# Router of a mixture-of-experts layer: rows scaled and turned by transposes, matmuls of 256 and 320 columns, ranks inside the shared block, gather behind the selectors

## The reference, cut to what matters

```
h = rms_norm_2(x, g_ffn_norm) * (1.0 + scale_f) + shift_f
def moe_ffn(h, w_router, b_router, w_exp_gate, w_exp_up, w_exp_down, w_sh_gate, w_sh_up, w_sh_down):
    scores = jax.nn.sigmoid(xf @ w_router)                 # 256 tokens x 64 experts
    choice = scores + b_router
    group_score = top_k(choice by 8 groups of 8, 2).sum     # keep the 4 best groups
    expert_idx = top_k(choice inside the kept groups, 6)
    gate = scores[expert_idx] / their sum * 2.5
    ...
    # every expert block (64 experts, each 1024 -> 256 -> 1024)
    hb = silu(xb @ w_exp_gate[e]) * (xb @ w_exp_up[e]);  y = (hb @ w_exp_down[e]) * g
    shared = (silu(xf @ w_sh_gate) * (xf @ w_sh_up)) @ w_sh_down
    return shared + routed
```

## Time and profile before

| | us |
|---|---|
| median of 3 runs | 1116.52 |
| lowest and highest | 1115.83 and 1118.21 |
| the profiled execution | 1116.18 |
| its span, first to last instruction | 1114.5 |
| TensorE busy | 1060.0 (95%) |
| VectorE busy | 560.6 (50%) |
| ScalarE busy | 392.7 (35%) |
| GpSimd busy | 385.3 (35%) |
| mean granted clock | 0.978 |

### The profile page before, as it was taken

The page is one execution under the profiler, slowest core; times in us unless marked ns, Lnnn a source line. Parts: engine busy times, 40 slices in busy tenths (PEclk is TensorE's granted clock), DMA queues, the critical chain, the costliest instruction groups (busy, mean ns, idle before and its releaser), DMA issues. The chain is left out here.

```text
span 1114.5 us, 12957 instructions
## 1 busy us (share of the span) xinstructions
PE 1060.0 (95%) x5046; PEld 705.6 (63%) x5046; DVE 560.6 (50%) x986; ACT 392.7 (35%) x677; POOL 385.3 (35%) x309
## 2 busy tenths in 40 slices
PE   8999999899999799799999999999999999999993
PEld 7788887788788687687888445444545454444442
DVE  5999768857956776655664222222222222212214
...
GB/s 323 249 234 216 209 203 176 241 210 217 269 185 180 152 287 209 76 190 151 90 209 390 197 392 410 419 418 417 416 416 418 418 417 416 416 417 417 418 383 39
DMA packets 88189, 320.65 MB, mean 288 GB/s; under 512 B 6688, under 2 KB 7728, under 8 KB 71232
## 3 DMA queue, kind: packets, MB, share of 16 engines
...
HBM read 318.74 MB, written 1.05 MB: 287 GB/s over the span
## 5 line engine op out<-in xcount | busy, mean ns | idle before, releaser
L810 PE MATMUL ps<-hl,L 128*128 128x512 f32 (+1 forms) x1216 | 386.4, 399 | 10.4 <-DVE rlo L1625 5.4
L810 PEld LDWEIGHTS ps<-hl,L 128*128 128x128 f32 x1216 | 229.3, 192 | 61.5 <-issue 10.9
L1625 DVE TENSOR_TENSOR rlo<-ring,hl 128x1024 fp32r<-128x1024 f32 (+1 forms) x154 | 217.3, 1434 | 83.7 <-ACT hl L1251 82.9
L810 PE MATMUL ps<-rlo,L 128*128 128x512 f32 (+1 forms) x608 | 239.5, 394 | 0.0
L810 PE MATMUL ps<-slots_all,xe 128*64 128x512 f32 (+1 forms) x1056 | 226.9, 582 | 0.8 <-DVE rt L2416 0.8
L1251 ACT ACTIVATE hl<-ring 128x1024 fp32r<-128x1024 f32 (+1 forms) x154 | 159.4, 1055 | 159.4 <-PE ps L810 107.0
L799 POOL CAST two<-ident 64x128 fp32r<-64x128 f32 x64 | 18.9, 295 | 506.3 <-PE ps L810 504.8
L752 POOL TENSOR_SCALAR mring<-mring,st 128x512 f32<-128x512 f32 x84 | 178.6, 2126 | 1.6
L810 PEld LDWEIGHTS ps<-slots_all,xe 128*64 128x64 f32 x1056 | 73.9, 137 | 131.7 <-issue 128.5
L810 PEld LDWEIGHTS ps<-rlo,L 128*128 128x128 f32 x608 | 116.2, 191 | 24.6
L754 POOL TENSOR_TENSOR macc<-macc,mring 128x512 f32<-128x512 f32 x84 | 121.6, 1448 | 7.0
...
## 6 DMA issues: line engine op xcount, KB each, us to landing
...
```

The lines of the kernel that those rows point to most:

```text
L810: return e.matmul(o, l, r, start=start, stop=stop)
L1625: return e.tensor_tensor(o, a, b, op)
```

## The change: what it does

1. **Scaling and turning.** VectorE no longer makes a diagonal matrix. It scales the rows themselves (`scaled_rows`: `xp` = `R` times 1/rms, 128x1024 for each half), and TensorE turns `xp` with transposes in place of matmuls.
2. **Weights side by side.** The router's 64 columns and the first 192 columns of the shared gate lie in one slot (`"shared"`). The last 64 gate columns and the 256 up columns lie in a new tile `shb` of 320 columns. `route` now runs with 256 columns, `shared_rest` with 320. SyncE issues four loads in place of three, and one slot in place of three is used.
3. **Order on TensorE.** Half of the route of m = 0 stands before the turn of m = 1, the other half behind it. The turning back (`h3_back`) of m = 0 stands before the route of m = 1. The rank matmuls stand behind the first of the second half's 320-column matmuls. `gather(0)` directly follows the shared block, and the transposes of ranks, gates and shared activations stand behind it.
4. **Order on the readers.** ScalarE shifts m = 0 before it squares the last quarter of m = 1, and does the sigmoid of the scores before the copies of the second half. The Silu is split in three. VectorE forms the selectors `pp` right behind the ranks and the gates after them, and moves `shared_act` and the low parts around.

The diff, cut to its core:

```diff
@@ -155,7 +155,8 @@
-xp = place("xp", [128, 2, 1024], at=X1 + 24 * K)
+xp = place("xp", [128, 2, 1024], at=X1 + 16 * K)
+shb = place("shb", [128, 8, 320], at=X1 + 24 * K)
...
@@ -507,20 +506,20 @@
-aux("router", "a", 0)
+aux(("h3", 0, 0), "v", 5), aux(("h3", 0, 4), "v", 6)
+aux("router", "a", 4)
+aux(("h3", 1, 0), "v", 7), aux(("h3", 1, 4), "v", 0)
-for n, (j0, m) in enumerate((j0, m) for j0 in (0, 4) for m in range(2)):
-    aux(("h3", m, j0), "v", 4 + n)
-aux(("sT", 0), "a", 0), aux(("sT", 1), "a", 2)
-aux("rT", "a", 1), aux("gT", "v", 3)
-        aux(("g", g, k), "av"[k % 2], (k + 3) % 4)
+        aux(("g", g, k), "av"[k % 2], (k + 3) % 4 if g else 4 + k % 4)
+aux("rT", "a", 3), aux("gT", "v", 0)
+aux(("sT", 0), "a", 1), aux(("sT", 1), "a", 2)
...
@@ -690,14 +689,15 @@
+    w.wait_ge(pe_aux.sem, pe_aux.at[("km", 1, 4)])
+    e.dma_start(shb[:, :, 0:64], WSG[:, :, 192:256]).then_inc(shared_in, 16)
+    e.dma_start(shb[:, :, 64:320], WSU).then_inc(shared_in, 16)
-            if name == "router":
+            if name == "shared":
-            elif name in ("sg", "su"):
-                w.wait_ge(pe_aux.sem, pe_aux.at[("sh", 1)])
...
@@ -719,6 +719,10 @@
+        if loads2_of[i] == "shared":
+            dst = slot2("shared").rearrange("p (a b) -> p a b", a=8)
+            e.dma_start(dst[:, :, 0:64], WR).then_inc(shared_in, 16)
+            dst = dst[:, :, 64:256]
...
@@ -1078,42 +1082,44 @@
-    wr = slot2("router")[:, 0:512].rearrange("p (k n) -> p k n", k=8)
-    wsg, wsu = (slot2(n).rearrange("p (k n) -> p k n", k=8) for n in ("sg", "su"))
+    wrg = slot2("shared").rearrange("p (k n) -> p k n", k=8)
-        spread_tokens("h3T", m, lambda m, j: R[:, m, :].rearrange("p (f k) -> p k f", k=8)[:, j, :], DIAG2,
-                      lambda m, j0: w.wait_ge(xp_set, m + 1))
-    def route(b, m):
-        w.wait_ge(*here2("router"))
-        for k in range(8):
+        turn_tokens("h3T", m, lambda m, j: xp[:, m, :].rearrange("p (f k) -> p k f", k=8)[:, j, :],
+                    lambda m, j0: w.wait_ge(xp_set, m + 1))
+    def route(b, m, ks):
+        w.wait_ge(*here2("shared"))
+        w.wait_ge(shared_in, 48)
+        for k in ks:
-            x = mm(b[:, 64 * m:64 * m + 64], ht3[:, k, tok(m)], wr[:, k, :], k == 0, k == 7)
+            x = mm(b[:, 256 * m:256 * m + 256], ht3[:, k, tok(m)], wrg[:, k, :], k == 4, k == 3)
-    def shared_half(b, m, name, wt, o):
-        w.wait_ge(*here2(name))
-        for k in range(8):
-            x = mm(b[:, o:o + 256], ht3[:, k, tok(m)], wt[:, k], k == 0, k == 7)
+    def shared_rest(b, m, ks):
+        for k in ks:
+            x = mm(b[:, 0:320], ht3[:, k, tok(m)], shb[:, k, :], k == 0, k == 7)
+    def h3_back(m):
+        turn_tokens("h3", m, lambda m, j: ht3[:, j, tok(m)], lambda m, j0: wait_read(("h3T", m, j0)))
-    route(br, 0)
+    route(br, 0, (4, 5, 6, 7))
-    b0 = take(("sh", 0))
-    shared_half(b0, 0, "sg", wsg, 0)
-    taken(route(br, 1))
-    taken(shared_half(b0, 0, "su", wsu, 256))
-    turn("h3", lambda m, j: ht3[:, j, tok(m)], lambda m, j0: None)
+    route(br, 0, (0, 1, 2, 3))
+    h3_back(0)
+    taken(route(br, 1, (4, 5, 6, 7, 0, 1, 2, 3)))
+    h3_back(1)
+    taken(shared_rest(take(("sh", 0)), 0, range(8)))
-    shared_half(b1, 1, "sg", wsg, 0)
+    shared_rest(b1, 1, (0,))
...
@@ -1121,30 +1127,32 @@
-    taken(shared_half(b1, 1, "su", wsu, 256))
-    for m in range(2):
+    taken(shared_rest(b1, 1, range(1, 8)))
+    def turn_shared(m):
-    b = take("rT")
-    w.wait_ge(rk_set, 2)
-    for m in range(2):
-        x = tr(b[:, tok(m)], rkz[:, m].rearrange("p r e -> p (r e)"))
-    taken(x)
-    b = take("gT")
-    w.wait_ge(gt_set, 2)
-    for m in range(2):
-        x = tr(b[:, tok(m)], gtt[:, m].rearrange("p r e -> p (r e)"))
-    taken(x)
+    def turn_ranks():
+        b = take("rT")
+        w.wait_ge(rk_set, 2)
+        for m in range(2):
+            x = tr(b[:, tok(m)], rkz[:, m].rearrange("p r e -> p (r e)"))
+        taken(x)
+        b = take("gT")
+        w.wait_ge(gt_set, 2)
+        for m in range(2):
+            x = tr(b[:, tok(m)], gtt[:, m].rearrange("p r e -> p (r e)"))
+        taken(x)
-        wait_turned("h3")
+                wait_read(("h3", m, 4 * (k // 4)))
...
@@ -1187,7 +1195,7 @@
-        wait_read(("sT", 0), ("sT", 1), *aux_names[aux_dense - 4:aux_dense], *(("mod", c) for c in MOD_SUM["end"]))
+        wait_read("router", ("sT", 0), ("sT", 1), *(("g", 0, k) for k in range(4, 8)), *aux_names[aux_dense - 4:aux_dense], *(("mod", c) for c in MOD_SUM["end"]))
...
@@ -1543,32 +1554,37 @@
+    def h3_high(m):
+        for j0 in (0, 4):
+            aux_done(("h3", m, j0))
+            act(h3hl[:, 0, m, 128 * j0:128 * j0 + 512], bank(("h3", m, j0))[:, :], ACT.Copy).then_inc(th.sem, 1)
+    h3_shift(0)
-    h3_shift(0)
+    h3_high(0)
-    act(SC, bank("router")[:, 0:128].rearrange("p (m e) -> p m e", m=2), ACT.Sigmoid).then_inc(aux_a.sem, 1)
-    aux_done(("sh", 0))
-    act(sh_[:, 0, 0:256], bank(("sh", 0))[:, 0:256], ACT.Silu).then_inc(silu_a, 1)
-    for j0 in (0, 4):
+    br = bank("router")[:, :].rearrange("p (m e) -> p m e", m=2)
+    act(SC, br[:, :, 0:64], ACT.Sigmoid).then_inc(sc_set, 1)
+    h3_high(1)
+    act(sh_[:, :, 0:192], br[:, :, 64:256], ACT.Silu).then_inc(aux_a.sem, 1)
+    for m in range(2):
+        aux_done(("sh", m))
+        act(sh_[:, m, 192:256], bank(("sh", m))[:, 0:64], ACT.Silu).then_inc(silu_a, 1)
+    def turned_shared():
+        aux_done("rT")
+        act(rgt[:, 0, :], bank("rT")[:, 0:256], ACT.Copy).then_inc(aux_a.sem, 1)
+        aux_done("gT")
+        act(rgt[:, 1, :], bank("gT")[:, 0:256], ACT.Copy).then_inc(th_g, 1)
-            aux_done(("h3", m, j0))
-            act(h3hl[:, 0, m, 128 * j0:128 * j0 + 512], bank(("h3", m, j0))[:, :], ACT.Copy).then_inc(th.sem, 1)
-    aux_done(("sh", 1))
-    act(sh_[:, 1, 0:256], bank(("sh", 1))[:, 0:256], ACT.Silu).then_inc(silu_a, 1)
-    for m in range(2):
-        aux_done(("sT", m))
-        act(sh_[:, m, 512:768], bank(("sT", m))[:, 0:256], ACT.Copy).then_inc(aux_a.sem, 1)
-    aux_done("rT")
-    act(rgt[:, 0, :], bank("rT")[:, 0:256], ACT.Copy).then_inc(aux_a.sem, 1)
-    aux_done("gT")
-    act(rgt[:, 1, :], bank("gT")[:, 0:256], ACT.Copy).then_inc(th_g, 1)
+            aux_done(("sT", m))
+            act(sh_[:, m, 512:768], bank(("sT", m))[:, 0:256], ACT.Copy).then_inc(aux_a.sem, 1)
...
@@ -2263,11 +2280,18 @@
-    def diagonal2(m):
+    def scaled_rows(m):
-        tsc(DIAG2(m), ident[:, :], st[:, 70 + m:71 + m], None, ALU.mult, None).then_inc(xp_set, 1)
+        tsc(xp[:, m, :], R[:, m, :], st[:, 70 + m:71 + m], None, ALU.mult, None).then_inc(xp_set, 1)
+    def h3_low(m):
+        for j0 in (0, 4):
+            w.wait_ge(th.sem, th.at[("h3", m, j0)])
+            c = slice(128 * j0, 128 * j0 + 512)
+            tt(h3hl[:, 1, m, c], bank(("h3", m, j0))[:, :], h3hl[:, 0, m, c].bitcast(F32), ALU.subtract)\
+                .then_inc(aux_v.sem, 1)
...
@@ -2283,16 +2307,17 @@
-    diagonal2(0)
+    scaled_rows(0)
-    diagonal2(1)
+    scaled_rows(1)
-    w.wait_ge(*read("router"))
+    h3_low(0)
+    w.wait_ge(sc_set, 1)
...
@@ -2382,15 +2392,21 @@
+    h3_low(1)
+    wait_mine()
+    mine(e.reciprocal(st[:, 50:52], st[:, 48:50]))
+    wait_mine()
+    mine(tt(GT, GT, spread(st[:, 50:52], 64), ALU.mult))
+    wait_mine()
+    tsc(GT, GT, 2.5, None, ALU.mult, None).then_inc(gt_set, 1)
+    w.wait_ge(gt_set, 1)
+    e.tensor_copy(gtt[:, :, :, :], GT.unsqueeze(2).to_broadcast([128, 2, 2, 64])).then_inc(gt_set, 1)
+    shared_act(0)
-    w.wait_ge(th_g, 1)
-        .then_inc(aux_v.sem, 1)
```

More of the change, by code:

```diff
@@ L329, in pk @@
             return W.rearrange("(p k) n -> p k n", k=n)
-        load2("router", 8, pk(D["w_router_2"], 8))
-        load2("sg", 8, pk(D["w_sh_gate_2"], 8))
-        load2("su", 8, pk(D["w_sh_up_2"], 8))
+        WR, WSG, WSU = (pk(D[q], 8) for q in ("w_router_2", "w_sh_gate_2", "w_sh_up_2"))
+        load2("shared", 8, WSG[:, :, 0:192])
         def downs(E):
@@ L379, in two_blocks @@
         r2_set, sq2_a, rt2_v, rt2_a, xp_set = (sem(n) for n in ("r2_set", "sq2_a", "rt2_v", "rt2_a", "xp_set"))
+        shared_in, sc_set = sem("shared_in"), sem("sc_set")
         sel_set, gt_set, rk_set, cnt_set, silu_a, sh_v, pick, gate_set, sh_pe, comb, th_g, two_set = (sem(n) for n in (
@@ L448, in aux_tokens @@
                 aux((name, m, j0), by)
-        BY_TOKENS = ("mT", "hT", "mT2")
+        BY_TOKENS = ("mT", "hT", "mT2", "h3")
         def turn_order(name, groups):
@@ L1221, in _ @@
             gather(0)
+            turn_ranks()
+            turn_shared(0)
+            turn_shared(1)
             turn_p(0)
@@ L1584, in _ @@
             gathered(0)
+            turned_shared()
             silu(0)
@@ L2365, in shared_act @@
                 w.wait_ge(silu_a, m + 1)
-                tt(sh_[:, m, 0:256], sh_[:, m, 0:256], bank(("sh", m))[:, 256:512], ALU.mult).then_inc(aux_v.sem, 1)
-            shared_act(0)
-            for j0 in (0, 4):
```

(12 more changed lines are left out.)

10 lines of the change are left out of this document (removed).

## The result

The changed kernel took 1103.47 us, the median of 4 runs (1102.96 to 1103.65). The kernel before has a median of 1116.17 over its first three runs and one beside these. The ratio is 0.9891 with an interval of 0.986 to 0.9923. The profiled execution took 1103.31 us, with a span of 1101.6 us.

A forecast was written before the change was run, and what follows sets the result against it. The expert loop was taken as a fixed-length block starting at the first gate_up. Gains of 3.5 us before R and 3.9 after made 7.4, less 1.9 for the clock: 5.5 us, median 1111.0, range 1107.0 to 1113.8.

The forecast's parts named there:

- What bounds the kernel: Expert loop: a block of fixed length from the first gate_up at 623.97 us; the change's worth is that instruction's shift.
- Part two, R to the first gate_up: Router stage from the end of the scores' matmuls to the first gate_up: 20.35 us against 24.3, 3.9 us gained.
- R: End of the scores' matmuls on TensorE: forecast at 596.2 us in place of 599.7, 3.5 us earlier at full clock.
- The turn: TensorE's transposes of xp, ahead of the route: 0.24 us each, 1.9 us for 8; bounds 0.12 and 0.24.
- The scaling: VectorE's 128x1024 pass making xp: 1.2 us taken, hidden for m = 0, on the path for m = 1.
- The clock: Router stage, around the two new gaps: one low-clock stretch expected, about 1.9 us lost, leaving 5.5 of 7.4 us.
- The dense part: Stage ahead of the router stage on TensorE: its end taken as 581.59 us, from the profile before.
- full clock and cheap turns: Rival in the router stage: no low stretch and 0.12 us transposes, gain 9.3 us, 1107.2; chance 0.27 with full clock alone.

The follow-up runs named there:

- a4: Changed kernel with the transposes of shared activations, ranks and gates ahead of the first gather again, as before; 1104.46 us, ratio 0.9931 to the kernel before.
- a6: Changed kernel with all eight 320-column matmuls of the second half ahead of the rank matmuls; 1106.43 us, ratio 0.9936 to the kernel before.
- c1: Kernel before, its diagonal matmuls taking contiguous columns in place of every eighth (features permuted, another result); 1113.0 us, ratio 1.0005.
- a5: Changed kernel with ScalarE shifting m = 0 behind the last square, the root and the table load, as before; 1110.7 us, ratio 0.9977 to the kernel before.
- b1: Kernel before with the new turn alone: VectorE scales the rows, TensorE turns them by transposes; 1113.47 us, ratio 0.9999.
- a1: Changed kernel with rows turned by 8 float32 matmuls with a diagonal matrix again, no scaled rows; 1109.69 us, ratio 0.997 to the kernel before.
- a7: Changed kernel with 16 more transposes, which nobody reads, ahead of the first turn; 1106.1 us.

## Why the prediction was wrong

- **What bounds the kernel.** Right. The loop behind the first `gate_up` kept its length (490.3 to 490.5 us in the two kernels' five profiles), the slots were full, and the whole gain is the shift of that instruction.
- **Part two, R to the first gate_up.** Right: 20.35 us forecast, 20.24 measured. The 320-column matmul took 0.54 us, `SEL` came less than 0.1 us before it was needed, and the gather did not wait. a4 shows what the old order of the tail would cost (0.8 us), and a6 what ranks behind the whole block would (2.4).
- **The turn.** This step failed in size: "I take 0.24 us per transpose, as the row that shares the step". It took 0.12. The weight load with the step takes a transpose 193 ns, against 141 without it:

```profile
L818 PEld LDWEIGHTS ps<-ident,xp 128*128 128x128 f32 x16 | 2.0, 193 | 0.7 <-issue 0.6
L818 PEld LDWEIGHTS ps<-ident,ht 128*128 128x128 f32 x16 | 1.9, 141 | 0.2
```

  The prediction had set 335 ns against 141, and so had compared two things at once, the step and the kind of instruction. Against contiguous loads of a float32 matmul (191 ns in c1, and there too a row comes every 0.12 us) the step cost that matmul some 140 ns a load. It cost the transpose 50, which left the load no slower than those 191 ns. Why a transpose pays less for the step was not tested. Two turns, 1.8 us. I had the bound of 0.12, and gave it to a rival.
- **The scaling.** 1.2 us taken, 0.75 measured: 0.45 us. The Trainium skill (VectorE: DVE Perf Modes, the perf-mode tier table) had the direction right: it gives a float32 `tensor_scalar` in SBUF twice the rate of a `tensor_tensor`. This trace has 0.75 us for 1024 columns where a two-operand pass over as many took 1.23, 0.61 of it and not quite half.
- With 0.4 us of smaller terms, R came 12.0 us after the first turn in place of 14.6. The order of ScalarE, which the prediction counted as part of this chain, is what made it possible (a5).
- **The clock.** This step failed too: "I expect one low stretch there". No stretch came, which is 1.9 us of the forecast. The clock fell in all profiles with a gap of 2.03 us or more in the stage (the kernel before twice, b1, c1, a5), and in none of the ten with the new turn whose longest gap was 1.24 or 1.69. It fell in a1 with a gap of 1.69 behind 3.85 us of diagonal matmuls. Why there is not shown. The length of the gap is not the only way to sort these profiles. What lay from the start of the turn to the first wide matmul, narrow work and waits together, was 5.5 us in a1 and 6.6 in a5, where the clock fell, against 2.7 in the changed kernel and 4.5 in a7, where it stayed up. No run parts the two readings, so the cause of the low clock stays open. The rule of the Trainium skill (TensorE: Matmul & The Clock Gate, Part 4: PE-mode transpose) that transposes do not count as busy in the way matmuls do is not settled either. a7's clock stayed up, but the same 4.1 us of transposes and single-column matmuls in the dense part were followed by the low clock in 8 of 17 profiles.
- **The dense part.** I took 581.6 us as given. It is one draw of a scatter of 7 us. The sum against the one profiled execution was wrong there by 2.6 us, and the first runs of before lay high: 69 later ones beside the experiments have medians of 1112.8 to 1113.9, by chip.

Added up: the stage is 10.2 us shorter, not 5.5 (1.8 + 0.45 + 0.4 + 1.9 + 0.1 more). The 2.6 us of the dense part come on top, and by the scatter shown they are luck. A fair distance of the two kernels is 7 to 11 us (1106.6 and 1103.1 against 1113.5 and 1113.9 on the same chips). The case that came, full clock and cheap turns, had been named as a rival at 1107.2, with too little chance.
